# Hybrid retention block on eight cores: w_o scaling on one engine, ten row buffers and earlier loads in the merge and w_o stages

## The chip, the cores and the metric

The kernel runs on all 8 cores of one Trainium2 chip, each core working on its own half sequence with no exchange between cores. The metric is the device time in microseconds of the slowest core. A core has a matrix engine (TensorE, PE in the profile), a vector engine (VectorE, DVE), a scalar engine (ScalarE, ACT), GpSimd (POOL) and SyncE (SP), which here only issues DMAs.

## The reference, cut to what matters

```
u   = rmsnorm(x) * (1 + sc1) + sh1
q, k, v, og, cb, cc, cx, ga, gb = split(u @ w_in)
y_ret  = (silu(og) * groupnorm(retention(rot(q), rot(k), v))) @ w_ret_out
y_conv = (cb * causal_conv(cc * cx)) @ w_conv_out
merged = sigmoid(ga) * y_ret + sigmoid(gb) * y_conv
h   = x + g1 * (merged @ w_o)
u2  = rmsnorm(h) * (1 + sc2) + sh2
out = rmsnorm(h + g2 * (square(relu(u2 @ w_ff1)) @ w_ff2))
```

x is 4 x 4096 x 1024 in float32. Matrix products run in bf16, sums in float32. g1, sc2, sh2 and g2 are vectors of 1024 values for each sequence, computed from the conditioning vector c.

## The kernel before, in words

Each core has 2048 tokens of output: 16 row tiles of 128 tokens, or four token blocks (tb) of 512. Three large buffers X, Y and Z (8 x 2048 bf16 for each partition) hold activations with channels on partitions. Weights pass through a ring of six slots of 1024 x 512; their loads are issued on POOL's queue (line 238) when the PE has finished with a slot. One list of operations is written in program order; each engine runs its own operations in that order, and semaphore waits are derived from keys: an operation waits for the last writer of what it reads and for the readers and the writer of what it writes. An operation waits in this way for earlier ones of its own engine too, PE apart. PE and PSUM: 8 banks; in the stages here six of them rotate (n_banks 6), the other two (6 and 7) serve transposes.

The stages in order are: modulation vectors, the prefix state, short convolution, the first branch gate, retention (line 885 on), its swish gate (r2, L1042 and L1044), then the stages that the change touches, then the MLP.

The merge (y2_group, lines 1101 to 1120) runs over tb 0 to 3 and eight channel tiles j. One group is 8 matmuls of Y with the retention output weights, 8 matmuls of X with the gate weights, a sigmoid on ACT (L1115) into scr[0], the product on DVE (L1116) into scr[1], and the sum into Z on POOL (L1118). Each of its products takes one bank.

In token block 0 the row vectors are made too: row_prep (L431 to L437, DVE) and row_mm (L306 on PE, copies to G_t by ACT at L449) first give g1 as rows in G_t. wo_scale (L1121 to L1130) then multiplies one 1024 x 512 chunk of w_o in its ring slot by g1. It is called after group 5 for chunk 0 and after group 7 for chunk 1; each call has two instructions of 128 x 2048 elements (kh 0 and 1), which write the same key, so the second waits for the first. After group 0 of token block 1 a second row_mm overwrites G_t with g2.

The w_o stage goes by row tiles. O_step(t) does O_mm(t): for both chunks 8 matmuls, and a DVE sum with the x tile in its row buffer (L1150); then the square on ACT (L453, into Y), and the store of the row to h1s on SP's queue. For even t it scales rows t-2 and t-1 (O_scale: L457 on DVE, L460 on POOL, L464 on DVE), then it issues the load of a later x tile on SP's queue, and transposes a pair of channel tiles of an earlier group (O_tpart, L477 on PE; evictions to X at L485 on ACT or L489 on DVE). Row t uses the buffer scr[3 + t mod 6]; the load of row t + 4 is issued in step t, and those of rows 0 to 3 before the merge. O_steps 0 to 9 are called after odd groups j of token blocks 1 to 3; the steps 10 to 15 come after the merge. Four store keys are taken in turn, so the store of row t also waits for that of row t-4.

The MLP follows: relu on ACT (L1259) into the two halves of scr[6], square on POOL (L1262). The final norm's weights are loaded into scr[7] on SP's queue after the last store, then rows of h1s into scr[0] and scr[1]. The products of w_ff2 are kept in AR (h2a, L1278). Before the w_o stage AR (4096 float32 values for each partition) holds the rotary tables (("AR", 0) and ("AR", 1)), the retention state, its bf16 copy and the mask.

Of the kernel before, what the change touches and what calls it, by code (L numbers as in the profile page):

```python
# [11 lines left out]
ALU = mybir.AluOpType  # L12
# [127 lines left out]
def build_program(dumps=(), stop_after=None):  # L140
    nc = bass.Bass("TRN2", target_bir_lowering=False)
    S = Sched()

    def din(name, shape, dt=F32):
        return nc.dram_tensor(name, list(shape), dt, kind="ExternalInput").ap()

    x_main = din("x_main", [2048, 1024])
# [24 lines left out]
    h1s = nc.dram_tensor("h1s", [2048, 1024], F32, kind="Internal").ap()  # L172

    with ExitStack() as es:
        def sb(name, shape, dt=F32):
            return es.enter_context(nc.sbuf_tensor(name, list(shape), dt))
# [5 lines left out]
        AR = sb("AR", [128, 4096], F32)  # L182
# [3 lines left out]
        state_bf = AR[:, 3072:3584].bitcast(BF16)  # L186
        mask = AR[:, 3584:4096]
        G_t = sb("G_t", [128, 1024], F32)
        scr = [sb("scr%d" % i, [128, 1024], F32) for i in range(9)]
        PS = es.enter_context(nc.psum_tensor("PS", [128, 4096], F32))  # L190
        pa = [PS[:, i * 512:(i + 1) * 512] for i in range(8)]
# [34 lines left out]
        ST4 = [("state", h) for h in range(4)]  # L226

        def SK(i):
            return [("scr", i, 0), ("scr", i, 1)]

        def SH(i, h):
            return ("scr", i, h)
# [4 lines left out]
        def dma(q, out, in_, reads, writes, key):  # L237
            return S.op(q, lambda e: e.dma_start(out=out, in_=in_), reads=reads, writes=writes, dma_key=key)  # L238
# [47 lines left out]
        def ring_use():  # L286
            i = rstate["use"]
            assert i < rstate["load"], "ring underflow (too many resident chunks)"
            rstate["use"] += 1
            return ring_t[r_slot[i]], ("ring", r_slot[i])  # L290
# [53 lines left out]
        for k in R8:  # L344
            S.op("dve", lambda e, k=k: e.tensor_scalar(out=crep[:, k, :], in0=ones_bf[:, :], scalar1=csil[:, k:k + 1],
                                                      scalar2=None, op0=ALU.mult),
                 reads=["ones", "csil"], writes=[("crep", k)])
# [104 lines left out]
        def sq_stats(src, srckeys, junk, junkkeys, col):  # L452
            S.op("act", lambda e: e.activation(out=junk, in_=src, func=AF.Square, accum_out=ss[:, col:col + 1]),  # L453
                 reads=srckeys, writes=junkkeys + [("ss", col)])
# [8 lines left out]
        def scale_x(src, srckeys, dst, dstkeys, col):  # L463
            S.op("dve", lambda e: e.tensor_scalar(out=dst, in0=src, scalar1=rstd[:, col:col + 1], scalar2=None, op0=ALU.mult),  # L464
                 reads=srckeys + [("rstd", col)], writes=dstkeys)

        def halves(ap):
            return ap.rearrange("p (a m) -> p a m", a=2)
# [73 lines left out]
        def uT_key(g, k):  # L542
            return ("Z", 4 + 2 * (g % 2) + k // 4, k % 4)
# [98 lines left out]
        for t in range(16):  # L642
            g, i = t // 4, t % 4
# [15 lines left out]
            if t == 11:  # L659
                S.op("dve", lambda e: e.tensor_copy(out=uTh[:, :, :].rearrange("p (a b) m -> p a b m", a=2),  # L660
                                                    in_=Z[:, 6:8, :].rearrange("p a (b m) -> p a b m", b=4)[:, :, :, 510:512]),
                     reads=[uT_key(3, k) for k in R8], writes=["uTh"])
# [65 lines left out]
        for jg in range(2):  # L728
# [4 lines left out]
            for jj in range(4):  # L733
                for (slot, skey, off) in ((s_cc, k_cc, 0), (s_cx, k_cx, 8)):
                    for k in R8:
# [4 lines left out]
                                                               in1=zhalo[:, 0:8], op0=ALU.mult, op1=ALU.mult),  # L740
                 reads=[("pa", bh), "zh_a", "flagc"], writes=["zh_b"])
# [4 lines left out]
            for jj, tb in c_order:  # L746
# [16 lines left out]
                    if tb == 0:  # L763
                        S.op("dve", lambda e, zcur=zcur, jj=jj: e.tensor_copy(out=zcur[:, 0:2], in_=zhalo[:, 8 + jj * 2: 8 + jj * 2 + 2]),
                             reads=["zh_b"], writes=zk)
                    elif jg == 0:
                        S.op("dve", lambda e, zcur=zcur, jj=jj: e.tensor_copy(out=zcur[:, 0:2], in_=zsave[:, jj * 2:jj * 2 + 2]),
                             reads=[("zs", jj)], writes=zk)
                    else:
                        S.op("dve", lambda e, zcur=zcur, zprev=zprev: e.tensor_copy(out=zcur[:, 0:2], in_=zprev[:, 512:514]),  # L770
                             reads=SK(3 + 1 - zi), writes=zk)
                    S.op("dve", lambda e, zcur=zcur, ccs=ccs, bcx=bcx: e.tensor_tensor(out=zcur[:, 2:514], in0=pa[bcx], in1=ccs, op=ALU.mult),
                         reads=[("pa", bcx), SH(zi, 0)], writes=zk)
                    if jg == 0 and tb < 3:
                        S.op("dve", lambda e, zcur=zcur, jj=jj: e.tensor_copy(out=zsave[:, jj * 2:jj * 2 + 2], in_=zcur[:, 512:514]),
                             reads=zk, writes=[("zs", jj)])
                    S.op("act", lambda e, zcur=zcur, t0=t0, j=j: e.activation(out=t0, in_=zcur[:, 0:512], func=AF.Copy,
                                                                             scale=convw[:, j * 3:j * 3 + 1]),
                         reads=zk + ["convw"], writes=[SH(zi, 1)])
                    S.op("dve", lambda e, zcur=zcur, t0=t0, t1=t1, j=j: e.scalar_tensor_tensor(out=t1, in0=zcur[:, 1:513], scalar=convw[:, j * 3 + 1:j * 3 + 2],  # L780
                                                                                               in1=t0, op0=ALU.mult, op1=ALU.add),
                         reads=zk + [SH(zi, 1), "convw"], writes=[SH(2, zi)])
                    S.op("dve", lambda e, zcur=zcur, t0=t0, t1=t1, j=j: e.scalar_tensor_tensor(out=t0, in0=zcur[:, 2:514], scalar=convw[:, j * 3 + 2:j * 3 + 3],
                                                                                               in1=t1, op0=ALU.mult, op1=ALU.add),
                         reads=zk + [SH(2, zi), "convw"], writes=[SH(zi, 1)])
                    S.op("dve", lambda e, t0=t0, bcb=bcb, j=j, tb=tb: e.tensor_tensor(out=Y[:, j, tb * 512:(tb + 1) * 512], in0=pa[bcb], in1=t0, op=ALU.mult),
                         reads=[("pa", bcb), SH(zi, 1)], writes=[("Y", j, tb)])
                    n = c_groups[0]
# [78 lines left out]
        for h in range(4):  # L867
            b = 4 + h // 2
# [4 lines left out]
        for h2 in range(2):  # L873
            S.op("dve", lambda e, h2=h2: e.tensor_copy(out=state[:, h2 * 512:(h2 + 1) * 512], in_=pa[4 + h2]),
                 reads=[("pa", 4 + h2)], writes=[("state", 2 * h2), ("state", 2 * h2 + 1)])
            S.op("act", lambda e, h2=h2: e.copy(out=state_bf[:, h2 * 512:(h2 + 1) * 512], in_=state[:, h2 * 512:(h2 + 1) * 512]),
                 reads=[("state", 2 * h2), ("state", 2 * h2 + 1)], writes=[("state_bf", 2 * h2), ("state_bf", 2 * h2 + 1)])
# [243 lines left out]
        def wo_scale(n):  # L1121
            o_slots.append(ring_use())
            slot, skey = o_slots[n]
            gb = G_t[:, n * 512:(n + 1) * 512].unsqueeze(1).to_broadcast([128, 4, 512])
            for kh in range(2):
                S.op("dve" if kh == 0 else "pool",
                     lambda e, kh=kh: e.tensor_tensor(out=slot[:, kh * 4:(kh + 1) * 4, :], in0=slot[:, kh * 4:(kh + 1) * 4, :],  # L1127
                                                      in1=gb, op=ALU.mult),
                     reads=[skey, "G", ("G", 1)], writes=[skey])
# [3 lines left out]
        def oxs(t):  # L1133
            return Y[:, 2 * (t % 4):2 * (t % 4) + 2, (t // 4) * 512:(t // 4 + 1) * 512]

        def oxsK(t):
            return [("Y", 2 * (t % 4) + a, t // 4) for a in range(2)]

        def O_load(t):
            i = 3 + t % 6  # L1140
            dma("sp", scr[i][:, :], x_main[t * 128:(t + 1) * 128, :], [], SK(i), ("xt", i))
            o_x[t] = i

        def O_mm(t):
            xi = o_x[t]
            for n, (slot, skey) in enumerate(o_slots):
                b = nbank()
                for k in R8:
                    mm(pa[b], ("pa", b), Z[:, k, t * 128:(t + 1) * 128], [("Z", k, t // 4)], slot[:, k, :], [skey], k == 0, k == 7)
                S.op("dve", lambda e, n=n, b=b: e.tensor_tensor(out=scr[xi][:, n * 512:(n + 1) * 512], in0=pa[b],  # L1150
                                                               in1=scr[xi][:, n * 512:(n + 1) * 512], op=ALU.add),
                     reads=[("pa", b), SH(xi, n)], writes=[SH(xi, n)])
            sq_stats(halves(scr[xi][:, :]), SK(xi), oxs(t), oxsK(t), 32 + t)
            dma("sp", h1s[t * 128:(t + 1) * 128, :], scr[xi][:, :], SK(xi), [("h1s", t)], ("h1st", t % 4))

        def O_scale(t):
            rs_stats(32 + t, 2)
            for u in (t, t + 1):
                xi = o_x[u]
                scale_x(halves(scr[xi][:, :]), SK(xi), oxs(u), oxsK(u), 32 + u)  # L1160

        def O_tpart(g, kp):
            tpart([oxs(4 * g + i) for i in range(4)], [oxsK(4 * g + i) for i in range(4)], kp, 6 + kp % 2,
# [2 lines left out]
        def O_step(t):  # L1166
            O_mm(t)
            if t >= 2 and t % 2 == 0:
                O_scale(t - 2)
            if t + 4 < 16:  # L1170
                O_load(t + 4)
            q = t - 6
            if q >= 0:
                O_tpart(q // 4, q % 4)

        for t in range(4):
            O_load(t)
        o_next = [0]

# [65 lines left out]
        for mb in range(2):  # L1245
            bank_ctr[0] = 0
            for fc in range(8):
                s_w, k_w = ring_use()
                for ff in range(4):
                    f = fc * 4 + ff  # L1250
                    for tb2 in range(2):
                        tb = mb * 2 + tb2
                        b = nbank()
                        for k in R8:
# [5 lines left out]
                             reads=[("pa", b)], writes=[SH(6, ri)])  # L1260
                        dst = hid_ap(f, tb2 * 512, (tb2 + 1) * 512)
                        S.op("pool", lambda e, r=r, dst=dst: e.tensor_tensor(out=dst, in0=r, in1=r, op=ALU.mult),  # L1262
                             reads=[SH(6, ri)], writes=hid_keys(f, [tb2]))
# [5 lines left out]
            for fg in range(4):  # L1269
                slot, skey = ring_use()  # L1270
                for tt in range(8):
                    b = f_banks[tt]
# [4 lines left out]
                    if fg == 3:  # L1277
                        S.op("dve", lambda e, b=b, tt=tt: e.tensor_tensor(out=h2a[:, tt, :], in0=pa[b], in1=G_t[:, 0:512], op=ALU.mult),  # L1278
                             reads=[("pa", b), "G"], writes=[("h2a", tt)] + (["mask"] + ST4 + [("state_bf", h) for h in range(4)] + [("AR", 0), ("AR", 1)] if mb == 0 else []))
# [3 lines left out]
            for tt in range(8):  # L1283
                t = mb * 8 + tt
                xi = load_h1(t, 0)
                S.op("pool", lambda e, xi=xi, tt=tt: e.tensor_tensor(out=h2a[:, tt, :], in0=h2a[:, tt, :], in1=h1b[xi], op=ALU.add),  # L1286
                     reads=[("h2a", tt), h1k[xi]], writes=[("h2a", tt)])
                sumsq(h2a[:, tt, :], ("h2a", tt), 48 + t)
                xi = load_h1(t, 1)
                b = f_banks[tt]  # L1290
                for f in range(32):
# [3 lines left out]
                    if tt == 7 and f % 8 == 7:  # L1295
                        ring_rel(skey)
                S.op("dve", lambda e, b=b: e.tensor_tensor(out=gb_t, in0=pa[b], in1=G_t[:, 512:1024], op=ALU.mult),
                     reads=[("pa", b), "G"], writes=[SH(2, 1)])
                S.op("dve", lambda e, xi=xi: e.tensor_tensor(out=h1b[xi], in0=gb_t, in1=h1b[xi], op=ALU.add),
                     reads=[SH(2, 1), h1k[xi]], writes=[h1k[xi]])  # L1300
# [3 lines left out]
                     reads=[("ss", 48 + t), ("ss", col)], writes=[("var", 48 + t)])  # L1304
                S.op("dve", lambda e, t=t: e.tensor_scalar(out=var[:, 64 + t:65 + t], in0=var[:, 48 + t:49 + t], scalar1=1.0 / 1024,
                                                           scalar2=EPS, op0=ALU.mult, op1=ALU.add),
                     reads=[("var", 48 + t)], writes=[("var", col)])
                S.op("pool", lambda e, col=col: e.tensor_tensor(out=rstd[:, col:col + 1], in0=var[:, col:col + 1], in1=mhalf[:, 0:1], op=ALU.pow),
                     reads=[("var", col), "mhalf"], writes=[("rstd", col)])
                oi = 3 + tt % 3  # L1310
                S.op("dve", lambda e, tt=tt, oi=oi, col=col: e.scalar_tensor_tensor(out=scr[oi][:, 0:512], in0=h2a[:, tt, :], scalar=rstd[:, col:col + 1],
                                                                                    in1=fnw[:, 0:512], op0=ALU.mult, op1=ALU.mult),
                     reads=[("h2a", tt), ("rstd", col), SH(7, 0), SH(7, 1)], writes=[SH(oi, 0)])
                S.op("dve", lambda e, xi=xi, oi=oi, col=col: e.scalar_tensor_tensor(out=scr[oi][:, 512:1024], in0=h1b[xi], scalar=rstd[:, col:col + 1],
                                                                                    in1=fnw[:, 512:1024], op0=ALU.mult, op1=ALU.mult),
                     reads=[h1k[xi], ("rstd", col), SH(7, 0), SH(7, 1)], writes=[SH(oi, 1)])
# [70 lines left out]
```

How the kernel before makes its waits and increments, by code:

```python
            def run_engine(e, eng):  # L93
                seen = {}
                for o in self.ops[e]:
                    need = {}
                    for d in o.deps:
                        if d.dma_key is not None:
                            key, val = ("d", d.dma_key), d.dma_count
                        else:
                            if not needs_sem(d, o):
                                continue
                            key, val = ("e", d.eng), d.count
                        if val > need.get(key, 0):
                            need[key] = val
                    for key, val in need.items():
                        if seen.get(key, 0) >= val:
                            continue
                        seen[key] = val
                        eng.wait_ge(dsem[key[1]] if key[0] == "d" else esem[key[1]], val)
                    ins = o.fn(eng)
                    if o.dma_key is not None:
                        ins.then_inc(dsem[o.dma_key], 16)
                    elif o.signal:
                        ins.then_inc(esem[e], 1)
                if e == "sp":
                    for o in final_ops:
                        eng.wait_ge(dsem[o.dma_key], o.dma_count)
```

## Time and profile before

| | us |
|---|---|
| median of 3 runs | 1321.45 (1319.44 to 1321.9) |
| the profiled execution | 1315.84 |
| span of its slowest core (core 1) | 1314.3 |
| spans of its cores | 1299.8 to 1314.3 |
| PE busy | 1227.0 (93%) |
| DVE, ACT, POOL busy | 506.4, 436.8, 492.9 |

Positions in the trace are microseconds from the start of the span. A timeline row gives start, duration, engine, line, operation, what it writes and reads, how many instructions it merges, and in brackets the idle time before it with what ended it. The granted clock is a share of 2.4 GHz. The stretch of interest lies from about 680 (last retention work) to 880 (first MLP groups).

### The profile page before, as it was taken

How to read it: one execution, taken by the hardware profiler on the slowest of the kernel's cores; microseconds unless marked ns; L12 is line 12 of the kernel's file. 1: busy time of each engine (PE TensorE's matmuls, PEld its weight loads, DVE VectorE, ACT ScalarE, POOL GpSimd, SP SyncE). 2: the span in 40 equal slices, each digit the busy share in tenths (PEclk: the TensorE clock that was granted, in tenths of full speed). 3: DMA queues.
4: the chain of work that ended last, by engine and by line, in shares of the span. 5: the costliest groups of instructions: out<-in, count | busy, mean ns of one | idle time of the engine just before them, and what ended most of it. 6: DMA issues, size and time to landing. Idle time of an engine off the chain costs nothing.

```text
span 1314.3 us, 19099 instructions; the slowest of 8 cores (1299.8 to 1314.3 us)
## 1 busy us (share of the span) xinstructions
PE 1227.0 (93%) x6320; PEld 581.8 (44%) x6320; DVE 506.4 (39%) x949; ACT 436.8 (33%) x738; POOL 492.9 (38%) x503
## 2 busy tenths in 40 slices
PE   2487899999999999999899999989999999999997
PEld 0243444444444455555444444444444444444443
DVE  5455455677422157776216333420000451000145
ACT  2264354221211147777531222333320113331011
POOL 1367100000000058887656222246640136663012
PEclk9789999999999999999999999999999999999999
DMA  9868900486765140000681332995454549945223
GB/s 175 215 159 169 156 6 1 64 122 80 106 79 64 24 58 1 1 2 1 108 134 17 96 112 81 212 200 87 75 86 66 112 152 173 140 65 86 51 92 125
DMA packets 86017, 123.31 MB, mean 94 GB/s; under 512 B 4640, under 2 KB 69152, under 8 KB 85920
## 3 DMA queue, kind: packets, MB, share of 16 engines
q0 software_dynamic: 67632, 70.26, 39.0%
q1 hardware_dynamic: 15984, 43.43, 10.4%
q10 hardware_dynamic: 2304, 8.39, 1.7%
q8 instruction: 53, 0.87, 0.3%
q14 instruction: 44, 0.36, 0.1%
HBM read 175.54 MB, written 16.78 MB: 146 GB/s over the span
## 4 chain that ended last, share of the span: by engine, by line
PE 84%; DMA 5%; DVE 3%; issue 2%; ACT 2%; POOL 2%; SPq 1%; DVEq 0%; POOLq 0%; ACTq 0%
PE PS L306 82%; DMA ring<-w_in 4%; PE PS L477 1%; DMA scr<-x_main 1%; DMA h1s<-scr 1%; ACT X L485 1%; SPq L238 1%; POOL ring L1127 0%; DVE AR L980 0%; PE PS L1018 0%; ACT Z L485 0%; DVE scr L437 0%; POOL grs L993 0%; POOL Z L1118 0%; PE PS L942 0%
## 5 line engine op out<-in xcount | busy, mean ns | idle before, releaser
L306 PE MATMUL PS<-X,ring 128*128 128x512 bf16 x2560 | 572.3, 381 | 10.6 <-ACT scr L1042 6.2
L306 PEld LDWEIGHTS PS<-X,ring 128*128 128x128 bf16 x2560 | 250.1, 98 | 311.8 <-issue 19.8
L306 PE MATMUL PS<-ring,Z 128*128 128x512 bf16 x896 | 208.2, 387 | 12.7 <-DMA ring<-w_in 7.7
L306 PEld LDWEIGHTS PS<-ring,Z 128*128 128x128 bf16 x896 | 88.3, 99 | 120.8 <-issue 23.3
L1278 DVE TENSOR_TENSOR AR<-PS,G_t 128x512 f32<-128x512 f32 x16 | 11.1, 692 | 294.9 <-PE PS L306 294.9
L1259 ACT ACTIVATE scr<-PS 128x512 f32<-128x512 f32 x128 | 76.2, 597 | 145.3 <-PE PS L306 90.1
L306 PE MATMUL PS<-Y,ring 128*128 128x512 bf16 x512 | 121.2, 382 | 0.0
L306 PE MATMUL PS<-ring,X 128*128 128x512 bf16 x512 | 117.8, 379 | 2.0 <-DVE AR L980 2.0
L306 PE MATMUL PS<-ring,Y 128*128 128x512 bf16 x512 | 113.4, 379 | 0.0
L1262 POOL TENSOR_TENSOR Z<-scr 128x512 bf16<-128x512 f32 x64 | 66.2, 1039 | 43.4 <-ACT scr L1259 38.0
L1262 POOL TENSOR_TENSOR Y<-scr 128x512 bf16<-128x512 f32 x64 | 66.6, 1041 | 36.9 <-ACT scr L1259 31.3
L306 PEld LDWEIGHTS PS<-Y,ring 128*128 128x128 bf16 x512 | 50.2, 99 | 60.2 <-issue 2.1
L306 PEld LDWEIGHTS PS<-ring,Y 128*128 128x128 bf16 x512 | 50.1, 98 | 60.5
L1118 POOL TENSOR_TENSOR Z<-scr,Z 128x512 bf16<-128x512 f32 x32 | 40.9, 1282 | 94.3 <-DVE scr L1116 88.6
L306 PEld LDWEIGHTS PS<-ring,X 128*128 128x128 bf16 x512 | 47.8, 98 | 55.2 <-issue 5.3
L460 POOL TENSOR_TENSOR rstd<-var,mhalf 128x2 f32<-128x2 f32 x24 | 17.5, 729 | 136.4 <-DVE var L457 136.2
L1116 DVE TENSOR_TENSOR scr<-PS,scr 128x512 f32<-128x512 f32 x32 | 21.9, 690 | 113.1 <-ACT scr L1115 69.8
L1240 ACT ACTIVATE scr<-AR 128x512 f32<-128x512 f32 x16 | 10.1, 630 | 162.7 <-POOL AR L1286 102.0
L238 POOL DMA_DIRECT2D ring<-w_in x17 | 15.5, 912 | 120.2 <-PE PS L306 120.2
L238 POOL DMA_DIRECT2D ring<-w_ff x32 | 29.3, 917 | 76.7 <-PE PS L306 76.7
L841 DVE TENSOR_TENSOR Z<-PS,scr 128x512 bf16<-128x512 f32 x32 | 22.1, 692 | 87.2 <-ACT scr L837 46.5
L306 PE MATMUL PS<-ring,crep 128*128 128x512 bf16 x96 | 28.6, 452 | 27.3 <-DMA ring<-w_ada 19.7
(164 smaller groups left out, 1345.0 us busy)
## 6 DMA issues: line engine op xcount, KB each, us to landing
ring<-w_ff POOLq DMA_DIRECT2D x32, 1024.0 KB, 8.5
ring<-w_in POOLq DMA_DIRECT2D x17, 1024.0 KB, 19.9
scr<-x_main SPq DMA_DIRECT2D x29, 512.0 KB, 6.1
ring<-w_ada POOLq DMA_DIRECT2D x12, 1024.0 KB, 12.1
h1s<-scr SPq DMA_DIRECT2D x16, 512.0 KB, 3.5
scr<-h1s SPq DMA_DIRECT2D x32, 256.0 KB, 4.7
y<-scr ACTq DMA_DIRECT2D x16, 512.0 KB, 4.6
scr<-x_pre SPq DMA_DIRECT2D x8, 512.0 KB, 13.8
```

The costliest lines, as they stand in the source:

```text
L238: return S.op(q, lambda e: e.dma_start(out=out, in_=in_), reads=reads, writes=writes, dma_key=key)
L306: S.op("pe", lambda e: e.matmul(out, lhsT, rhs, start=start, stop=stop), reads=list(lkeys) + list(rkeys), writes=[okey])
L460: S.op("pool", lambda e: e.tensor_tensor(out=rstd[:, col:col + n], in0=var[:, col:col + n], in1=mhalf[:, 0:n], op=ALU.pow), reads=[("var", ...
L477: S.op("pe", lambda e, k=k, kk=kk, ti=ti: e.transpose(ptb[b][:, kk * 512 + ti * 128:kk * 512 + (ti + 1) * 128], blk(srcs[ti], k), ident[:, ...
L485: S.op("act", lambda e, src=src, dst=dst, k=k: e.activation(out=dst, in_=src, func=AF.Identity, scale=mT[:, sc + k:sc + k + 1], bias=mT[:, ...
L841: S.op("dve", lambda e, sg=sg, by=by, dst=dst: e.tensor_tensor(out=dst, in0=pa[by], in1=sg, op=ALU.mult), reads=[("pa", by), SH(0, si)], w ...
L1116: S.op("dve", lambda e: e.tensor_tensor(out=tm, in0=pa[by], in1=sg, op=ALU.mult), reads=[("pa", by), SH(0, si)], writes=[SH(1, si)])
L1118: S.op("pool", lambda e: e.tensor_tensor(out=dst, in0=tm, in1=dst, op=ALU.add), reads=[SH(1, si), ("Z", j, tb)], writes=[("Z", j, tb)])
L1240: S.op("act", lambda e: e.activation(out=junk, in_=src, func=AF.Square, accum_out=ss[:, col:col + 1]), reads=[key], writes=[SH(2, 0), ("ss ...
L1259: S.op("act", lambda e, r=r, b=b: e.activation(out=r, in_=pa[b], func=AF.Relu), reads=[("pa", b)], writes=[SH(6, ri)])
L1262: S.op("pool", lambda e, r=r, dst=dst: e.tensor_tensor(out=dst, in0=r, in1=r, op=ALU.mult), reads=[SH(6, ri)], writes=hid_keys(f, [tb2]))
L1278: S.op("dve", lambda e, b=b, tt=tt: e.tensor_tensor(out=h2a[:, tt, :], in0=pa[b], in1=G_t[:, 0:512], op=ALU.mult), reads=[("pa", b), "G"], ...
```

## The change

Four things are edited. Both instructions of wo_scale run on DVE. The row buffers are ten: scr[3] to scr[8] and the four quarters of AR, with the keys of the tables, the state and its bf16 copy with the mask; row t uses buffer t mod 10. The load of row t + 8 is issued in step t, and the loads of rows 0 to 7 before the merge. The sum L1150 now reads and writes the keys of the whole row buffer and not of its half.

```
-                S.op("dve" if kh == 0 else "pool",
+                S.op("dve",
...
+        ob = [scr[3 + i][:, :] for i in range(6)] + [AR[:, i * 1024:(i + 1) * 1024] for i in range(4)]
+        obk = [SK(3 + i) for i in range(6)] + [[("AR", 0)], [("AR", 1)], list(ST4), [("state_bf", h) for h in range(4)] + ["mask"]]
+
         def O_load(t):
-            i = 3 + t % 6
-            dma("sp", scr[i][:, :], x_main[t * 128:(t + 1) * 128, :], [], SK(i), ("xt", i))
+            i = t % 10
+            dma("sp", ob[i], x_main[t * 128:(t + 1) * 128, :], [], obk[i], ("xt", i))
             o_x[t] = i
...
-                S.op("dve", lambda e, n=n, b=b: e.tensor_tensor(out=scr[xi][:, n * 512:(n + 1) * 512], in0=pa[b],
-                                                               in1=scr[xi][:, n * 512:(n + 1) * 512], op=ALU.add),
-                     reads=[("pa", b), SH(xi, n)], writes=[SH(xi, n)])
-            sq_stats(halves(scr[xi][:, :]), SK(xi), oxs(t), oxsK(t), 32 + t)
-            dma("sp", h1s[t * 128:(t + 1) * 128, :], scr[xi][:, :], SK(xi), [("h1s", t)], ("h1st", t % 4))
+                S.op("dve", lambda e, n=n, b=b: e.tensor_tensor(out=ob[xi][:, n * 512:(n + 1) * 512], in0=pa[b],
+                                                               in1=ob[xi][:, n * 512:(n + 1) * 512], op=ALU.add),
+                     reads=[("pa", b)] + obk[xi], writes=obk[xi])
+            sq_stats(halves(ob[xi]), obk[xi], oxs(t), oxsK(t), 32 + t)
+            dma("sp", h1s[t * 128:(t + 1) * 128, :], ob[xi], obk[xi], [("h1s", t)], ("h1st", t % 4))
...
-                scale_x(halves(scr[xi][:, :]), SK(xi), oxs(u), oxsK(u), 32 + u)
+                scale_x(halves(ob[xi]), obk[xi], oxs(u), oxsK(u), 32 + u)
...
-            if t + 4 < 16:
-                O_load(t + 4)
+            if t + 8 < 16:
+                O_load(t + 8)
...
-        for t in range(4):
+        for t in range(8):
             O_load(t)
```

## Rows read from the trace of the kernel before

**Rows 1.** The page, busy us (share of the span) and instructions of each engine.

```profile
PE 1227.0 (93%) x6320; PEld 581.8 (44%) x6320; DVE 506.4 (39%) x949; ACT 436.8 (33%) x738; POOL 492.9 (38%) x503
```

**Rows 2.** View of cores: span and mean granted clock.

```profile
core 0: 1307.4 us, clock 0.980
core 1: 1314.3 us, clock 0.980
...
core 3: 1311.7 us, clock 0.977
```

**Rows 3.** Waits of PE, 700 to 880: who for whom, us, times, longest.

```profile
PE PS L477 <- ACT X L485: 3.5, 1, 3.5
PE PS L306 <- POOL ring L1127: 2.5, 1, 2.5
```

**Rows 4.** Timeline of PE at the first w_o products.

```profile
712.07 1.89 PE L306 MATMUL PS<-Y,ring 128*128 128x512 bf16 x8
...
715.52 1.89 PE L306 MATMUL PS<-ring,Z 128*128 128x512 bf16 x8
719.95 2.40 PE L306 MATMUL PS<-ring,Z 128*128 128x512 bf16 x8 [2.54 <-POOL ring L1127]
```

**Rows 5.** Timeline of DVE in the same stretch.

```profile
703.39 2.94 DVE L1127 TENSOR_TENSOR ring<-ring,G_t 128x2048 bf16<-128x2048 bf16 x1
706.25 0.68 DVE L1116 TENSOR_TENSOR scr<-PS,scr 128x512 f32<-128x512 f32 x1
709.00 0.69 DVE L1116 TENSOR_TENSOR scr<-PS,scr 128x512 f32<-128x512 f32 x1 [2.07 <-PE PS L306]
709.61 3.93 DVE L1127 TENSOR_TENSOR ring<-ring,G_t 128x2048 bf16<-128x2048 bf16 x1
```

**Rows 6.** Timelines of POOL in the same stretch.

```profile
703.02 1.16 POOL L1118 TENSOR_TENSOR Z<-scr,Z 128x512 bf16<-128x512 f32 x1 [6.54 <-DVE scr L1116]
...
707.30 4.08 POOL L1127 TENSOR_TENSOR ring<-ring,G_t 128x2048 bf16<-128x2048 bf16 x1
711.35 3.20 POOL L1118 TENSOR_TENSOR Z<-scr,Z 128x512 bf16<-128x512 f32 x1
```

**Rows 7.** Timeline of ACT: the second copies to G_t, and the first relus.

```profile
719.84 1.26 ACT L449 COPY G_t<-PS 128x512 f32<-128x512 f32 x2 [7.70 <-POOL ring L1127]
...
867.99 1.09 ACT L1259 ACTIVATE scr<-PS 128x512 f32<-128x512 f32 x2 [9.34 <-DMA h1s<-scr]
```

**Rows 8.** Timeline of PE in the first MLP groups.

```profile
863.40 3.62 PE L306 MATMUL PS<-X,ring 128*128 128x512 bf16 x16
870.56 0.69 PE L477 MATMUL PS<-ident_s,Y 128*128 128x128 bf16 x8 [3.54 <-ACT X L485]
871.09 5.30 PE L306 MATMUL PS<-X,ring 128*128 128x512 bf16 x16
```

**Rows 9.** Windows: us; busy of PE, PEld, DVE, ACT, POOL; clock, DMA share, GB/s.

```profile
684.00:692.00 8.00, 8.00 (x39) 3.64 (x38) 5.78 (x20) 1.54 (x3) 1.14 (x1) 1.00 1.06 170
715.00:727.00 12.00, 9.46 (x37) 3.76 (x35) 2.23 (x4) 2.82 (x5) 6.97 (x4) 0.86 0.21 66
866.00:880.00 14.00, 10.46 (x53) 4.78 (x52) 0.99 (x2) 7.73 (x13) 9.58 (x10) 0.88 1.09 193
```

**Rows 10.** The window of wait A on core 0, PE alone.

```profile
715.00:727.00 12.00, 9.26 (x43) 1.00 0.18 50
```

**Rows 11.** The window of wait B on core 3, PE alone.

```profile
855.00:880.00 25.00, 22.09 (x139) 1.00 1.09 224
```

**Rows 12.** Timeline of PE: an earlier stall, late in retention.

```profile
636.87 3.61 PE L306 MATMUL PS<-X,ring 128*128 128x512 bf16 x16 [2.11 <-ACT scr L1042]
```

**Rows 13.** Row 13's store: its issue on SP's queue; KB each, us to landing.

```profile
848.42 0.33 SPq L238 DMA_DIRECT2D h1s<-scr  x1
...
h1s<-scr SPq DMA_DIRECT2D x1, 512.0 KB, 12.2
```

**Rows 14.** DMA issues of 680 to 682: KB each, us to landing.

```profile
ring<-w_o POOLq DMA_DIRECT2D x1, 1024.0 KB, 13.2
scr<-x_main SPq DMA_DIRECT2D x2, 512.0 KB, 5.9
```

**Rows 15.** All DMA issues of 700 to 1100, time to landing.

```profile
DMA to landing us min/median/max: 2.7/8.1/37.2
```

## Prediction

> **What bounds the kernel now.** I read the page's table of engines first: PE is busy 93% of the span and no other engine over 40% [rows 1]. So an edit moves the time only where PE waits for the work edited, or where its clock falls. The view of cores comes next, since the time is that of the slowest core: core 1, with cores 3 and 0 behind it [rows 2]. Third, the waits of PE alone, from the last retention work to the start of the MLP: there are two, 2.5 us for the w_o scaling (L1127) and 3.5 us for an ACT eviction of the transposes [rows 3]. After 880 us PE waits for nothing. The kernel's x loads, L1150 sums and stores lie beside full PE work elsewhere in this stretch.
>
> Wait A. PE has the first half of row tile 0's w_o product at 715.52 and starts the second only at 719.95 [rows 4]. The second half needs w_o's second chunk scaled. Its scaling was a chain: DVE half at 709.61 for 3.93 us, then POOL's half of about 4.08 us behind a queued merge sum [rows 5, 6]. The ACT copy into G_t waits 7.70 us for the same POOL instruction [rows 7]. After the stall the clock of 715 to 727 us is 0.86, a mix of the levels 2.4 and 1.2 GHz, so 12 x 0.14 = 1.7 us more are lost [rows 9]. Core 0 has the same stall and keeps 1.00 [rows 10].
>
> Wait B. The MLP's first relu writes scr[6], where row tile 15 lives (3 + 15 mod 6). ACT waits 9.34 us for the store of that tile [rows 7]. PE runs on until its six banks are full, near 867.0 (863.40 plus 3.6), then waits until 870.56; its next sixteen matmuls take 5.30 us where sixteen usually take 3.62 [rows 8]; the clock of 866 to 880 is 0.88, and 14 x 0.12 is the same 1.7 us [rows 9]. That is 3.54 + 1.68 = 5.2 us on core 1. Core 3 loses 25 - 22.09 = 2.9 us here at full clock [rows 11].
>
> **The change, part by part.** 1. The last quarter-chunks of the scaling go from POOL to DVE. The two POOL instructions of 4.08 us go. What a DVE half costs by itself comes out of the starts: the first begins at 703.39 while POOL's add of 703.02 runs until 704.18, and ends at 706.33, that is 2.15 us after the add; the second begins at 709.61, POOL is busy until 711.35, and it ends at 713.54, again 2.19 us later [rows 5, 6]. So it is a 2.2 us instruction, and DVE and POOL take turns here. POOL's add shows the other side: 3.20 us beside the DVE half and 1.16 without [rows 6].
>
> The new DVE order is half, half, evict (0,6), evict (0,7), half, half, evict (1,0); (t,j) is a group of the merge. Starting from 706.33, and giving POOL's waiting add the turn between two halves: 706.33 + 1.16 + 2.2 = 709.7; two evictions of 0.69, started 0.61 apart, reach 711.0 [rows 5]. The add of (0,6) then runs until about 711.6, a half until 713.8, the add of (0,7) until 714.9, the last half until 717.1, and the eviction of (1,0) until 717.8. Banks rotate by six, so w_o's first product of tile 0 takes the bank that (1,0) leaves. PE is ready for it at 715.5 [rows 4]: a stall of 2.3 us, earlier, instead of 2.54. If DVE's second half goes first in each gap, the evictions wait only for (0,7)'s data (709.00 + 0.7 [rows 5]), the halves end near 714.7, (1,0) leaves at 715.4, and no stall remains. If a DVE half costs what POOL's does, 4.08, scaling ends at 706.33 + 4.1 + 1.3 + 8.2 = 719.9 and PE starts at 720.6: a stall of 5.1, 2.6 worse than now, with the clock loss kept. So part 1 lies between a gain of 2.5 + 1.7 = 4.2 and a loss of 2.6. I take the first chain, since POOL's add is already waiting at each gap: 0.2 us of stall. The clock is open: it kept 2.4 GHz through a stall of 2.11 us [rows 12] and mostly fell after 2.5. 2.3 is between, so I take half of 1.7. Part 1: 1.1 us.
>
> A rule is to be weighed here. The DVE half's length beside POOL is the shared thing, and the rows show turns, not a slower pace. The Trainium skill (SBUF — State Buffer, Who interferes with whom) says that a DVE instruction with two SBUF inputs contends with a GpSimd one that reads SBUF, and that the first to issue holds the ports for its whole length. By it the chain is the one above, and the trace agrees (2.15 and 2.19 us left after POOL's end). Were it a shared bandwidth instead, the halves would stay at 2.94 and 3.93 us, w_o's product would start near 719, and part 1 would lose 1.1 us.
>
> The covers of part 1: the ACT copies to G_t (L449) now follow the last DVE half at about 717.1, not 719.7, so the sigmoid of (1,1) behind them is earlier too. Both second-row matmuls need the bank of (0,6), free at 710.4, when they begin just after 711.2: covered by 0.8 us.
>
> 2. Ten row buffers. Row 15 goes to buffer 5 (scr[8]), and scr[6] holds row 13. In the trace row 13's store is issued at 848.42 and lands 12.2 us later, at 860.6 [rows 13]. The first relu can start at about 858.7, when the last square of ACT is done, so it would wait 2 us, not 9.34. PE is only held if the relus and transposes' eviction (2.5 us) end after 867.0, which is a landing after 864.4; 860.6 leaves 3.8 us. Wait B goes: 5.2 us on core 1, 2.9 on core 3, nothing on core 0. Late next is nothing on PE: the transposes of rows 12 to 15 need DVE's scale of row 15, done before 862.
>
> Row 14 goes to scr[7], into which the final-norm weights are loaded. That load on SP's queue and the h1s reads behind it now wait for row 14's store and scale, some 4 us later. The first h1s read is used only after the w_ff2 products, beyond 1000 us: cost nothing while that cover stands. The AR rows replace rotary tables, state and mask, whose last readers ended before 640; h2a takes AR over after 1000. The sum of the second half of a row (L1150) now also waits for the first half's: both on DVE, 1.7 us apart, so nothing, or 0.1 us where they run back to back off PE's path.
>
> 3. Loads eight ahead. Eight SP issues before the merge in place of four: the third and all after wait for scr[5], as now, so six 512 KB loads leave at 681 in place of two. Behind them on SP is only the store of row 0 at 723. They share the DMA engines with w_o's second chunk, issued at 681 too and landed after 13.2 us, at 694.2 [rows 14]. Four more loads are 2.1 MB; at the 170 GB/s of 684 to 692 [rows 9] that is 12.3 us, were all of it to fall on the chunk: 706.5. The scaling wants it at 711.0, covered by 4.5 us. Later, loads t+8 wait for row t-2's scale and store, just the distance of t+4 into six buffers, with the same store behind them. The last load goes out near 798 in place of 841, which takes 1 MB from the crowded stretch of the last stores: a gain for part 2, not counted.
>
> **The sum** on core 1: 5.2 + 1.1 = 6.3 us, 1314.3 to 1308.0. Core 3: 1311.7 - 2.9 - 1.1 = 1307.7. Core 0 has no B and no clock loss: 1307.4 - 0.2 = 1307.2. Core 1 stays slowest by little. The profiled execution took 1315.84 (span 1314.3 and 1.5 around it) and would take 1309.5. The median of the runs is 1321.45, 5.6 above it; the same 6.3 off gives 1315.1.
>
> **The rivals.** R1, both waits vanish with the clock kept: 4.2 + 5.2 = 9.4, 1312.0. For it: POOL is freed of 8.2 us; against: the adds still take their turns. R2, DVE's halves are as dear as POOL's: 5.2 - 2.6 = 2.6, 1318.8; against it are the two ends at 2.15 and 2.19. R3, only part 1 counts: either row 13's store lands after 864.4 because the w_ff chunks take the engines, or the slowest core of most executions is one without B, as core 0 here: 1.1, 1320.3. For it: B differs from core to core, 0 to 5.2 us; against: the slowest two here have it. R4, slower: the burst of six loads holds w_o's second chunk. DVE's half waits in order, and the eviction of (1,0) behind it. POOL being idle by then, PE restarts 4.4 + 0.7 = 5.1 us after the landing L. The stall is L + 5.1 - 715.5, plus 1.7 of clock; it eats A's 4.2 and B's 5.2 from L = 718.1, 37 us after issue. A landing in this kernel took up to 37.2 us [rows 15]; that would be the same as before, and 43 us would be 1327. Against it: it needs nearly three times the 13.2 us.
>
> **How the numbers follow.** Forecast 0.58 (1315.1, own range 1313 to 1317.5), R1 0.12, R2 0.08, R3 0.14, R4 0.08. This kernel's runs lie within 0.2% (2.6 us), which is what can be told from no change, so 1318.8 to 1324.1 is the same. R2 lies on that edge and is split. Faster: 0.58 + 0.12 + 0.04 = 0.74; same: 0.04 + 0.14 = 0.18; slower 0.08. The range leaves out R4 and part of R3 above, and a little below R1's value for a slowest core with a larger B: 1311 to 1319.8.
>
> **What would show it.** In the profile after: four DVE instructions of L1127, 2.2 to 3.4 us each; PE's wait there moves to the first w_o matmul, at 2.3 us or less, released by DVE; the ACT relu's wait on the store under 3 us, no wait of L477 on ACT, and clock 1.00 from 855 on. Wrong would be: DVE halves at 4 us, a wait for w_o's load, a relu wait past 864, or a slowest core that is late before 700 and had no B.

## The result, and the profile after

| | before | changed |
|---|---|---|
| median of 5 runs, first session | 1319.44 (1317.15 to 1321.9) | 1309.77 (1308.82 to 1311.72) |
| profiled execution | 1315.84 | 1309.52 |
| span of its slowest core | 1314.3 (core 1) | 1308.1 (core 7) |

The ratio is 0.9924 (95% interval 0.9904 to 0.9944): 9.7 us between the medians, where 6.3 was forecast. In a later session it was 0.9943 (0.9930 to 0.9955), about 7.5 us. In the later sessions some executions ran with a lower clock on one die; the ratios leave them out, and medians of those sessions are not given below.

First the waits of PE on the slowest core of the changed kernel, 640 to 900 us (who for whom, us, times, longest). They answer to [rows 3].

```profile
PE PS L306 <- DVE scr L1116: 2.0, 2, 1.7
```

Neither old wait is left. One of 1.7 us has come, for an eviction of the merge. The timeline of PE shows its place; [rows 4] was the place before.

```profile
715.08 1.89 PE L306 MATMUL PS<-X,ring 128*128 128x512 bf16 x8
718.68 3.61 PE L306 MATMUL PS<-ring,Z 128*128 128x512 bf16 x16 [1.70 <-DVE scr L1116]
```

The sixteen w_o matmuls run through now; before, the stall cut them in half. The timelines of DVE and POOL answer to [rows 5] and [rows 6]:

```profile
704.62 6.09 DVE L1127 TENSOR_TENSOR ring<-ring,G_t 128x2048 bf16<-128x2048 bf16 x2
710.64 1.28 DVE L1116 TENSOR_TENSOR scr<-PS,scr 128x512 f32<-128x512 f32 x2
711.84 6.09 DVE L1127 TENSOR_TENSOR ring<-ring,G_t 128x2048 bf16<-128x2048 bf16 x2
717.85 0.68 DVE L1116 TENSOR_TENSOR scr<-PS,scr 128x512 f32<-128x512 f32 x1
```

```profile
704.25 4.32 POOL L1118 TENSOR_TENSOR Z<-scr,Z 128x512 bf16<-128x512 f32 x2 [6.56 <-DVE scr L1116]
711.46 4.32 POOL L1118 TENSOR_TENSOR Z<-scr,Z 128x512 bf16<-128x512 f32 x2 [2.89 <-DVE scr L1116]
```

The first add begins 0.37 us before the first half, so the order is add, half, add, half. The two halves take 6.09 us with the end of one add and the whole of the next; POOL's two adds take 4.32, two times 1.16 and once 2.0 of waiting. The next rows are ACT's copy to G_t and its first two relus, for [rows 7].

```profile
718.07 1.26 ACT L449 COPY G_t<-PS 128x512 f32<-128x512 f32 x2 [4.64 <-DVE ring L1127]
...
856.89 0.60 ACT L1262 ACTIVATE scr<-PS 128x512 f32<-128x512 f32 x1 [0.64 <-PE PS L306]
858.08 0.60 ACT L1262 ACTIVATE scr<-PS 128x512 f32<-128x512 f32 x1 [0.59 <-PE PS L477]
```

The relu waits for PE alone, not for a store. The windows that stood at 0.86 and 0.88 in [rows 9] now read:

```profile
715.00:727.00 12.00, 10.30 (x49) 4.59 (x47) 6.00 (x6) 3.42 (x6) 3.09 (x3) 1.00 0.26 84
866.00:880.00 14.00, 14.00 (x88) 7.14 (x85) 1.99 (x4) 6.99 (x12) 8.38 (x9) 1.00 1.11 188
```

Last the DMA issues of 679 to 690, for [rows 14]: KB each, median us to landing.

```profile
scr<-x_main SPq DMA_DIRECT2D x4, 512.0 KB, 8.7
ring<-w_o POOLq DMA_DIRECT2D x1, 1024.0 KB, 17.9
AR<-x_main SPq DMA_DIRECT2D x2, 512.0 KB, 12.9
```

With six x loads beside it and not two, w_o's chunk took 17.9 us here against 13.2 (16.3 to 19.7 on the eight cores, against 10.1 to 13.4). It was issued at 682.2, so it landed at 700.1, and its scaling began at 711.8.

**A measure that leaves the start out.** In one execution the cores reach the first scaling instruction at different times, 11 us apart here (693.7 to 704.6) and 24 us in e1, and this scatter is larger than the effect. I therefore take for each core the span minus the start of its first L1127, and call it the tail. A row of the view of line L1127 gives the start, here 704.6 on the slowest core of the changed kernel (duration min/median/max in ns, then the first and the last start); before it was 703.39 [rows 5].

```profile
L1127 DVE TENSOR_TENSOR ring<-ring,G_t x4: 2928/2996/3058, 704.6 to 714.9; 128x2048 bf16<-128x2048 bf16 x4
```

So 1308.1 - 704.6 = 603.5, and 1314.3 - 703.4 = 610.9. All runs by this measure, one profiled execution of eight cores each (e5 to e8 have no other execution, and so no ratio):

| run | tail, us | stall A, us | its clock kept | wait B, us |
|---|---|---|---|---|
| before, profiled execution | 603.9 to 611.4 | 2.5 to 2.7 | 1 of 8 | 0 to 3.9 |
| e5, before again | 605.9 to 610.7 | 2.5 to 2.7 | 3 of 8 | 0.4 to 3.7 |
| e6, before a third time | 607.0 to 611.8 | 2.4 to 2.5 | 3 of 8 | 1.4 to 4.1 |
| changed | 603.4 to 603.5 | 1.7 to 1.9 | 8 of 8 | 0 |
| e9, changed again | 603.6 to 603.9 | 1.9 to 2.1 | 8 of 8 | 0 |
| e1, DVE scaling alone | 603.0 to 607.3 | 1.8 to 2.0 | 8 of 8 | 0 to 3.4 |
| e2, rotation alone | 603.9 to 605.6 | 2.4 to 2.5 | 1 of 8 | 0 |
| e3, ten buffers, POOL scaling | 604.2 to 605.9 | 2.2 | 3 of 8 | 0 |
| e8, the same, four ahead | 605.2 to 606.9 | 2.5 to 2.7 | 1 of 8 | 0 |
| e7, changed, row 15 in scr[6] | 605.0 to 611.1 | 1.7 to 1.9 | 8 of 8 | 1.3 to 5.1 |
| e10, rotation and DVE scaling | 602.8 to 602.9 | 1.7 to 1.9 | 8 of 8 | 0 |
| e4, changed, halves apart | 601.6 to 601.8 | 0 | 8 of 8 | 0 |
| e12, the same again | 601.6 to 601.9 | 0 | 8 of 8 | 0 |
| e11, e10 with halves apart | 601.4 to 601.5 | 0 | 8 of 8 | 0 |

Stall A is PE's wait at the first w_o products, wait B its wait of L477 on ACT at the start of the MLP. "Its clock kept" counts the cores on which the granted clock was 1.00 from 8 to 32 us after the start of the scaling; on all others it was 0.93 there, which is 24 x 0.07 = 1.7 us.

### The profile page after: what moved, and what is told of

It reads as the page before. It is cut to its first block, busy times and chain, and to the rows that moved or that the text cites. A ratio compares the mean times of both kernels' runs of the same rounds, so it can differ in the third digit from the quotient of the medians.

```text
span 1308.1 us, 19081 instructions; the slowest of 8 cores (1297.1 to 1308.1 us)
## 1 busy us (share of the span) xinstructions
PE 1222.8 (93%) x6320; PEld 580.6 (44%) x6320; DVE 513.1 (39%) x951; ACT 437.1 (33%) x738; POOL 485.8 (37%) x501
## 4 chain that ended last, share of the span: by engine, by line
PE 86%; DMA 5%; DVE 2%; ACT 2%; issue 2%; POOL 1%; SPq 1%; DVEq 0%; POOLq 0%; ACTq 0%
PE PS L306 84%; DMA ring<-w_in 4%; PE PS L477 1%; DMA scr<-x_main 1%; SPq L238 1%; ACT X L485 1%; PE PS L1018 0%; DVE AR L980 0%; ACT Z L485 0%; DVE scr L437 0%; POOL Z L1118 0%; ACT scr L1004 0%; PE PS L945 0%; PE PS L942 0%; POOL ring L238 0%
## 5 line engine op out<-in xcount | busy, mean ns | idle before, releaser
L1118 POOL TENSOR_TENSOR Z<-scr,Z 128x512 bf16<-128x512 f32 x32 | 40.9, 1282 | 99.4 <-DVE scr L1116 95.9
L1243 ACT ACTIVATE scr<-AR 128x512 f32<-128x512 f32 x16 | 10.1, 630 | 162.4 <-POOL AR L1289 102.0
## 6 DMA issues: line engine op xcount, KB each, us to landing
ring<-w_in POOLq DMA_DIRECT2D x17, 1024.0 KB, 16.3
scr<-x_pre SPq DMA_DIRECT2D x8, 512.0 KB, 16.3
```

Of the source, the lines that this page charges most:

```text
L1118: S.op("pool", lambda e: e.tensor_tensor(out=dst, in0=tm, in1=dst, op=ALU.add), reads=[SH(1, si), ("Z", j, tb)], writes=[("Z", j, tb)])
```

## The experiments

**Part 1 alone** (e1_dve_scaling), the kernel before with:

```
-                S.op("dve" if kh == 0 else "pool",
+                S.op("dve",
```

> Part 1 alone: the kernel before with both halves of each w_o scaling on DVE; six row buffers and loads four ahead stay. Theory T1 (the two waits add up; wait A was worth 0.8 us of stall and 1.7 us of clock, wait B 0 to 5.6 us by core): the stall at the first w_o product is 1.7 us with the clock kept; the store of row 15 still holds the first relu, so each core keeps its own wait B; the time from the first scaling instruction to the end of the core is 2.5 us shorter than before plus B, 603.5 + B on every core. Ratio to before about 0.998. Rival T2 (most of the gain comes from the loads eight ahead): the same here. Rival T3 (the adds on POOL, freed of 8.2 us, were worth more than the stall): ratio 0.996 or less.

Ratio 0.9998 (0.9960 to 1.0037): the interval holds the forecast of 0.998 and no change alike. In the profiled execution cores 0 to 3 had a granted clock of 0.92 to 0.94 before the scaling, cores 4 to 7 had 0.97 to 0.98, and the cores reached the scaling between 691.7 and 716.0. The tail leaves this out. The stall is 1.8 to 2.0 us, the clock 1.00 after it on all cores, and wait B is still there on seven of them. These are PE's waits on core 2:

```profile
PE PS L477 <- ACT X L485: 3.4, 1, 3.4
PE PS L306 <- DVE scr L1116: 2.1, 2, 1.8
```

Without B's share the tails are 603.0 to 603.4 where the clock was kept throughout, against 606 with stall A and its clock loss. T1 holds: part 1 is worth about 2.5 us on a core that lost its clock at stall A (2.4 from e3 to the changed kernel, 2.8 from e2 to e10). The larger gain of T3 does not show in the tails.

**The rotation alone** (e2_rotation), the kernel before with:

```
-            i = 3 + t % 6
+            i = 3 + (t + 2) % 6
```

> Wait B alone, by the smallest edit: six row buffers as before, but row t uses scr[3 + (t + 2) mod 6], so row 15 lies in scr[8] and scr[6] holds row 13. POOL scaling and loads four ahead stay. T1: no wait of the transposes on ACT at the MLP's start on any core; stall A of 2.5 to 2.7 us stays with its clock loss, 606 us from the first scaling instruction to the end on every core (603.5 + 2.5); ratio 0.995 or so, as the two slowest cores lose 3 to 5 us of wait. T2 (the loads eight ahead matter): row 13's store lands late beside the x loads, the relu waits past 864 and 1 to 3 us of wait B stay.

Ratio 0.9956 (0.9921 to 0.9991). No core has wait B, here core 1, and stall A is as before:

```profile
PE PS L306 <- POOL ring L1127: 2.5, 1, 2.5
PE PS L306 <- DVE scr L1116: 0.3, 1, 0.3
```

Seven cores have a tail of 605.4 to 605.6; core 3 kept its clock and has 603.9. The windows of the stall on core 1 and on core 3 show that difference of 1.7 us:

```profile
714.00:726.00 12.00, 9.48 (x37) 0.86 0.20 62
```

```profile
706.00:718.00 12.00, 9.48 (x44) 1.00 0.24 80
```

So one number in one line removes wait B, without more buffers and with the loads still four ahead.

**The change without part 1** (e3_ten_buffers_pool): the changed kernel with `"dve" if kh == 0 else "pool"` again.

> The change without part 1: ten buffers and loads eight ahead, one half of each scaling on POOL as before. T1: the same as the rotation alone within 1 us (606 us from scaling to end, ratio 0.995). T2: faster than the rotation alone by 2 us or more, ratio 0.993 or less, since this would be the part that carries the gain.

Tails of 605.8 to 605.9 with the clock loss and 604.2 without, the rotation's own plus 0.3. The ratio, 0.9978 (0.9948 to 1.0008), overlaps the rotation's. T2 falls: the early loads carry no gain.

**Ten buffers, loads four ahead** (e8_ten_four_ahead): the run before with `t + 4` and four first loads.

> Ten buffers, one half of each scaling on POOL, loads only four ahead. T1: like the six buffers turned by two and like ten buffers with loads eight ahead, 605.6 to 605.9 us from scaling to end where the clock falls once and 603.9 to 604.2 where it does not; no wait of L477 on ACT. T2: one or more cores show a wait B of over 0.5 us.

No wait B on any core, and six tails of 605.8 to 605.9, as forecast. Core 7 has 606.9, and core 6, which kept its clock at stall A, has 605.2, each 1 us more than forecast. No wait of PE explains it; the windows do. In the MLP the clock fell on these two cores, here core 7 and then, for comparison, core 5:

```profile
1080.00:1090.00 10.00, 10.00 (x43) 0.89 1.10 191
```

```profile
1080.00:1090.00 10.00, 10.00 (x48) 1.00 1.11 195
```

That is 10 x 0.11 = 1.1 us, with PE busy all the time. So the clock was also seen to fall where PE had no wait; why it did is open. With these 1.1 us taken off, all eight tails are as T1 had them.

**Row 15 in scr[6] again** (e7_row15_in_scr6), the changed kernel with:

```
-            i = t % 10
+            i = (t + 8) % 10
```

> The changed kernel with the ten buffers turned so that row 15 lies in scr[6] again (buffer (t + 8) mod 10); loads eight ahead and DVE scaling stay. T1 (wait B is the store of row 15 standing before the first relu, wherever the loads are): wait B comes back on several cores, 0.2 to 3 us, somewhat less than before since 1 MB of x loads has left the stretch; 603.5 plus that wait to the end. T2 (the early loads empty the queue and let the store land in time): the ACT wait is under 3 us and PE has no wait, 603.5 on all cores.

Wait B is back on all eight cores, and not smaller than before as T1 had it: 1.3 to 5.1 us, where the three executions of before have 0 to 4.1. On core 3, the waits of PE, then that of ACT:

```profile
PE PS L477 <- ACT X L485: 5.1, 1, 5.1
PE PS L306 <- DVE scr L1116: 1.7, 1, 1.7
```

```profile
ACT scr L1262 <- DMA h1s<-scr: 12.1, 1, 12.1
```

The x loads are gone from this stretch, and ACT still waits 12.1 us for the store of row 15 (9.34 on core 1 before [rows 7]). This is one execution. The traffic left beside it is the w_ff chunks and the stores ahead of it; which of them delays it was not tried. The clock fell too, to 0.83 in a window of 19 us, which is 3.2 us:

```profile
855.00:861.00 6.00, 2.52 (x12) 0.96 1.07 224
861.00:880.00 19.00, 17.33 (x94) 0.83 0.96 150
```

**Before, twice more** (e5_before_again and e6_before_third).

> The kernel before once more, for the spread of wait B over executions. T1 says that the time after the first scaling instruction is 606.1 plus the stall and the clock loss of wait B on each core, and that B differs from core to core and from execution to execution between 0 and 6 us. If the slowest core of most executions has B at 4 us or more, the change is worth more on the median than the 6.3 us that the two profiled executions show; if B on the slowest core averages 3 us, the rest of the measured 9.7 us lies before the scaling, in where the slowest core arrives.

> The kernel before a third time, same reading: PE's wait of L477 on ACT by core, 0 to 4 us, and 604 to 611 us from the first scaling instruction to the end.

The 24 tails of before have a mean of 608.7; those of the slowest cores are 610.9, 609.9 and 609.5, against 603.5. The slowest core's tail thus gains 6.0 to 7.4 us. The executions took 1315.84, 1316.28 and 1316.67.

**The changed kernel again** (e9_changed_again) **and the two causes alone** (e10_rotation_and_dve: the edits of e1 and e2 together), in one session.

> The changed kernel again, beside runs of the kernel before in the same session. From the executions so far: 603.5 us from the first scaling instruction to the end on every core; before has 607 to 612 there. T1: the slowest core gains 6 to 7.5 us, ratio 0.9945 to 0.995; a ratio under 0.993 in undisturbed runs would mean that the change also moves something before the scaling.

> The two causes alone: six row buffers turned by two, both scaling halves on DVE; loads four ahead, keys by half row, no AR buffers. T1: the same time as the changed kernel (603.2 us from scaling to end, ratio to before equal within 0.1%), so that the ten buffers and the early loads carry nothing. T2: the changed kernel is faster by 1 us or more.

Ratios 0.9943 (0.9930 to 0.9955) and 0.9945 (0.9930 to 0.9959): the same time from two edited lines. In the tail the small version is ahead, 602.8 to 603.6. Some of it stands at the very end, where DVE starts the last product (L1314, L1311 there) 1.02 us after POOL's last instruction began in the changed kernel and 0.65 us in e10, with operations and shapes alike; why was not found.

**The stall that is left.** PE waits for the eviction of merge group (1,0), which stands behind two halves on DVE. e4_split_halves is the changed kernel with:

```
-                        wo_scale((j - 5) // 2)
+                        wo_scale((j - 5) // 2, (0, 1) if j == 5 else (0,))
...
                     if tb == 1 and j == 0:
+                        wo_scale(1, (1,))
                         row_mm(scr[2][:, :], SK(2))
```

> The changed kernel with the last scaling half moved in program order to after the first merge group of token block 1, so that the eviction of that group stands ahead of it on DVE. T1 (the 1.7 us stall that is left comes from the bank that this eviction frees): the first w_o product starts without a wait, the second one waits for the last half at most 0.3 us, and 601.8 us pass from the first scaling instruction to the end; ratio to before about 0.991. Rival (the halves' own length sets the time): PE waits the same 1.7 us, now for the scaling, and the time is that of the changed kernel.

PE has no wait left in the stage (core 2; PE, then DVE):

```profile
713.42 1.89 PE L306 MATMUL PS<-X,ring 128*128 128x512 bf16 x8
715.14 3.62 PE L306 MATMUL PS<-ring,Z 128*128 128x512 bf16 x16
```

```profile
710.17 2.93 DVE L1128 TENSOR_TENSOR ring<-ring,G_t 128x2048 bf16<-128x2048 bf16 x1
713.03 0.68 DVE L1116 TENSOR_TENSOR scr<-PS,scr 128x512 f32<-128x512 f32 x1
713.63 2.64 DVE L1128 TENSOR_TENSOR ring<-ring,G_t 128x2048 bf16<-128x2048 bf16 x1
```

The eviction ends at 713.7, before PE needs its bank at 715.14, and the last half at 716.3, before the second eight matmuls. Ratio 0.9907 (0.9868 to 0.9945), tail 601.6 to 601.8. e12 repeats it and e11_minimal_split makes the same move in e10.

> The changed kernel with the last scaling half moved, again, in a session with the others: 601.6 us from scaling to end on every core as in the first run of it, ratio to before 0.993, equal to the small version within 0.1%.

> As the run before, with the last scaling half behind the first merge group of token block 1. T1: 1.7 to 2 us better again, 601.4 us from scaling to end, no wait of PE there; ratio to before about 0.993. Rival: without the ten buffers the x tile's load is late for a sum and DVE holds PE's bank; then it is behind the ten-buffer version.

Ratios 0.9943 (0.9923 to 0.9963) for e12, from two runs, and 0.9932 (0.9916 to 0.9948) for e11. The tails agree to 0.3 us with the forecast and on all cores, some 2 us under the changed kernel. In total time the intervals overlap with that of the changed kernel; only the tails put e11 ahead of both kernels.

## Why the prediction was right or wrong

**Wait A, the chain: right.** It put the eviction of (1,0) at 717.8, 14.4 us after the first half's start at 703.39; it ended 13.9 us after it. A stall of 2.3 us was forecast and 1.7 came. The halves are 2.2 us instructions that take turns with POOL's adds; that a DVE half costs what POOL's does (4.08 us, the prediction's R2) did not come. By the Trainium skill (SBUF — State Buffer, Who interferes with whom) the engine that issues first holds the port; the trace agrees, with 6.09 us for two halves, the end of one add and the whole of the next. The shared-bandwidth reading gave a start of w_o's product near 719; it came at 718.68 with the scaling 1.2 us later than before, so at about 717.5 on the old scale, 0.3 us from the 717.8 of the turns, and that reading falls.

**Wait A, the clock: the mis-sized term.** I took half of 1.7 us since 2.3 lay between a stall that kept the clock and one that mostly did not. The stall came under that bound, and the clock was kept on every core, so the whole 1.7 us returned wherever it had been lost. Part 1 measured about 2.5 us, not 1.1. In the sum for core 1 this is the term that was too small: 6.3 us were forecast, and its tail gained 7.4.

**Wait B: right.** The cause was the store of row 15 in scr[6], 5.2 us on core 1; e2 removes it alone and e7 brings it back. One sentence of the prediction on it was not borne out: that the departure of the x loads helps part 2. In e7 no help shows, and by e8 it isn't needed.

**The covers: right.** w_o's chunk landed at 700.1, between the 694.2 of before and the bound of 706.5. Nothing waits for the norm weights in scr[7], and PE never waited for an x tile.

**The sum: right by luck in part.** The profiled execution was put at 1309.5 and took 1309.52. But core 1 was to be slowest at 1308.0; with the tail as measured it would have been 703.4 + 603.5 = 1306.9. A core that came 1.2 us later to the scaling, core 7, made up the difference.

**The step that failed is the last one**, "the same 6.3 off gives 1315.1". It carried the 5.6 us between the profiled execution and the median of three runs of before over to the changed kernel. Those 5.6 us were no property of the kernel: two further runs took the median to 1319.44, three profiled executions took 1315.84 to 1316.67, and nine runs of a later session 1312.0 to 1317.5. In the session of e1 to e4 the 22 runs of before that count took 1311.5 to 1329.4: the level of one and the same kernel moves by more than the offset that was carried over. The changed kernel's profiled execution was 0.25 us from its median. With all of the runs, the change is worth 6.0 to 7.4 us on the tail of the slowest core and 7.5 in the later session. The 9.7 of the first session has 2.3 to 3.7 us more than the tails explain. They must lie before the scaling or in a larger B of those unprofiled runs; which one is open, as only profiled executions show where a core lost its time. One part of that stretch can be left out: from the first merge sum (L1118) to the first scaling instruction it took 17.9 to 18.1 us on every core of the three executions of before and the two of the changed kernel, although the four additional x loads run there. Ahead of it nothing was changed. The range ended at 1311.0, 1.2 us above the time, because its low end was built from the terms of the sum alone and held nothing for the base.

## What to carry to other kernels

When a buffer is handed from one stage to the next, ask which of the last tiles lives in the one that the next stage writes first: turning the rotation by two did what four more buffers did. An engine's half of a shared operation may cost less on the engine that already holds the other half, but count what is queued behind it: the eviction of a bank was worth 1.7 us. With scatter of several us between cores, measure from an instruction that all cores pass just ahead of the edit, and base a forecast in absolute us on the level of several executions and its scatter, not on one median of three.

## What the runs showed of the hardware that was not expected

The clock's answer to a stall at this place is a matter of tenths of a microsecond. In 40 core records with a stall of 2.4 to 2.7 us here it fell on 31 and was kept on 9; at 2.2 us (e3) it fell on 5 of 8; at 1.7 to 2.1 us it was kept on all 40. A fall cost 1.7 us each time. The 40 short stalls stand eight matmuls earlier than the others, so by these records alone the place could count as well as the length. Wait B settles that, as it has one place in all runs: in the five executions that have it, the clock was kept on all 16 cores with a wait of 0.2 to 2.1 us and fell on 20 of the 22 with 2.3 to 5.1 us (kept at 2.9 in the profiled execution of before and at 3.4 in e1). So the last half microsecond of a stall can be worth three times its length.
